# Hybrid decoder step on one core: expert stage fed by quarter rows, transposed on VectorE, multiplied contraction-outer

## What is computed

```python
# per token: one group of 4, then the best 2 of its 8 experts -> 2 x 1088 = 2176 rows to compute
def block(args):
    tok, e = args                      # a block of slots that share one expert
    xb = h[tok]                        # gather rows of 1024 floats
    return (jax.nn.silu(xb @ w1[e]) * (xb @ w3[e])) @ w2[e]    # 1024 -> 512 -> 1024
out = lax.map(block, (slot_tok.reshape(nb, MOE_BLOCK), block_exp))
y = zeros.at[slot_tok].add(out.reshape(-1, D_MODEL) * slot_w[:, None])
```

## Time and profile before

| what | us |
|---|---|
| runs shown, median | 1646.29 |
| the profiled execution, first to last instruction | 1641.5 |
| up products of the first block begin | 997.1 |
| last down product ends | 1585 |
| the next stage's first DMA | 1603.4 |

### The profile page before, as it was taken

The page is one execution under the profiler, slowest core; times in us unless marked ns, Lnnn a source line. Parts: engine busy times, 40 slices in busy tenths (PEclk is TensorE's granted clock), DMA queues, the critical chain, the costliest instruction groups (busy, mean ns, idle before and its releaser), DMA issues. The chain is left out here.

```text
span 1641.5 us, 34661 instructions
## 1 busy us (share of the span) xinstructions
PE 1487.8 (91%) x14240; PEld 979.1 (60%) x14240; DVE 538.9 (33%) x1270; ACT 435.9 (27%) x1227; POOL 290.5 (18%) x250
## 2 busy tenths in 40 slices
PE   8999999989998999999999857999999999999950
PEld 4666666657566677777777433566666655555530
DVE  2445544413325544455444360111111111111106
ACT  2211111131123344434443100222222222222224
POOL 0000000002124333343333001111111111111115
PEclk9999999989998999999999977999999999999985
DMA  7332233242316122221221187999999999999975
GB/s 257 87 94 70 67 81 81 55 147 82 108 63 247 33 78 103 88 99 46 78 84 40 64 350 275 350 384 375 380 377 371 384 368 384 385 378 382 381 265 217
DMA packets 120115, 334.71 MB, mean 204 GB/s; under 512 B 42808, under 2 KB 72424, under 8 KB 92648
## 3 DMA queue, kind: packets, MB, share of 16 engines
q1 hardware_dynamic: 111160, 306.88, 50.4%
q0 software_dynamic: 7728, 22.29, 5.8%
q10 hardware_dynamic: 1152, 4.52, 0.7%
HBM read 290.37 MB, written 48.14 MB: 206 GB/s over the span
## 5 line engine op out<-in xcount | busy, mean ns | idle before, releaser
L2191 PE MATMUL bank<-sb_arena 128*32 128x256 f32 x6336 | 357.3, 386 | 12.9 <-DMA sb_arena<-w 11.8
L398 PE MATMUL bank<-sb_arena 128*128 128x368 f32 x1056 | 330.6, 476 | 6.7 <-DMA sb_arena<-xT 6.7
L2191 PEld LDWEIGHTS bank<-sb_arena 128*32 128x32 f32 x6336 | 205.1, 112 | 153.9 <-DMA sb_arena<-w 13.8
L398 PEld LDWEIGHTS bank<-sb_arena 128*128 128x128 f32 x1056 | 201.7, 191 | 133.5 <-DMA sb_arena<-w_conv 6.7
L2214 PE MATMUL bank<-sb_arena 128*32 128x256 f32 x3168 | 177.1, 379 | 2.0 <-DMA sb_arena<-w 1.0
L2214 PEld LDWEIGHTS bank<-sb_arena 128*32 128x32 f32 x3168 | 102.7, 110 | 70.7 <-issue 2.5
L985 PE MATMUL bank<-sb_arena 128*128 128x512 f32 (+1 forms) x288 | 131.2, 595 | 6.3 <-DVE sb_rlog L1596 5.0
L2157 POOL DMA_INDIRECT d_acc<-sb_arena,sb_oidx x32 | 46.2, 1444 | 472.1 <-ACT sb_arena L2280 472.1
L2330 DVE SCALAR_TENSOR_TENSOR sb_arena<-sb_arena,bank 128x128 f32<-128x128 f32 x99 | 28.6, 288 | 297.3 <-ACT sb_arena L2266 297.3
L2266 ACT ACTIVATE sb_arena<-bank 128x128 f32<-128x128 f32 x99 | 27.5, 278 | 353.6 <-PE bank L2191 353.6
L782 PE MATMUL bank<-sb_arena 128*128 128x384 f32 (+1 forms) x288 | 96.5, 488 | 7.7 <-PEq L151 7.7
(11 more groups left out here) (346 smaller groups left out, 1750.0 us busy)
## 6 DMA issues: line engine op xcount, KB each, us to landing
sb_arena<-w SPq DMA_DIRECT2D x204, 1024.0 KB, 30.5
sb_arena<-w_conv SPq DMA_DIRECT2D x28, 512.0 KB, 4.7
sb_arena<-d_conv SPq DMA_DIRECT2D x7, 1792.0 KB, 7.3
d_conv<-sb_arena SPq DMA_DIRECT2D x22, 512.0 KB, 3.3
sb_arena<-d_gam SPq DMA_DIRECT2D x8, 768.0 KB, 4.1
d_x<-sb_arena SPq DMA_DIRECT2D x9, 512.0 KB, 2.6
sb_arena<-xT ACTq DMA_DIRECT2D x8, 552.0 KB, 9.6
sb_arena<-w_out SPq DMA_DIRECT2D x8, 512.0 KB, 7.0
```

The costliest lines, as they stand in the source:

```text
L398: last = e.matmul(bank[3 * r + s][:, 0:TN], wring[n % NV][:, k, :], xT[:, k, TN * s:TN * s + TN], start=(k == 0), stop=(k == KT - 1))
L2191: mm = e.matmul(bank[r][j * CG:(j + 1) * CG, 0:2 * P], xgT[:, k, g * CG:(g + 1) * CG], w13[s][quarter_of(j, r)][:, k, :], start=(k == 0), ...
```

## The change

**Rows.** A row of `d_x1` or `d_acc` is handled as four pieces of 1 KB. Partition 32*j + i of group r holds quarter j of slot 32*r + i. `xg` and `eo` become 128 partitions x 3 groups x 256. Each gather is three indirect DMAs of 128 pieces, each scatter is three as well, each of them waiting for its own third (`e_eo0` to `e_eo2`). The index table `slot` is spread over 128 partitions in the routing stage: 12 small products and four VectorE operations take the place of seven VectorE operations, and the value is 4 * row + quarter.

**Transposes.** VectorE transposes blocks of 32 x 32 from SBUF to SBUF: `x_flip` (128 x 768) and `h_flip` (128 x 384). TensorE's 11 transposes and ScalarE's three copies of each block go. The weights are laid out in DRAM to match the order of contraction that this gives.

**Products.** `up` runs over four pieces of w13, each of which is now a quarter of the contraction, and all three groups of rows are summed in three PSUM banks side by side; `e_up` counts quarters. `down` does the same with two halves of w2. Numbers and shapes of products are the same (96 and 48, 128 x 32 by 256). `tanh` and `gate` become one instruction each for all three groups, after the whole up product; the gate weight is applied at eviction. TensorE's step is `up(b)`, `down(b-1)`. VectorE's step is `x_flip(b+1)`, `take(b+2)`, `gate(b)`, `mark(b-1)`, `h_flip(b)`.

```diff
-                for ex in range(NSET, E):
-                    for q in (0, 1, 3, 2):
-                        e.wait_ge(S["e_up"], 3 * (ex - NSET) + min(q, 2) + 1)
+                for ex in range(NSET, E):
+                    for q in range(4):
+                        e.wait_ge(S["e_up"], 4 * (ex - NSET) + q + 1)
                         load13(q, ex % NSET, a["w13"][ex, q])
...
                 def gather(index):
                     e.wait_ge(S["e_go"], 1)
                     e.wait_ge(S["e_idx"], index)
-                    e.indirect_dma_start(xg[0:BLK], None, a["d_x1"], bass.IndirectOffsetOnAxis(ap=idx[:, 0:1], axis=0),
-                                         bounds_check=TO - 1, oob_is_err=False).then_inc(S["e_x"], 16)
+                    for r in range(NR):
+                        e.indirect_dma_start(xg[:, r, :], None, rows_in, bass.IndirectOffsetOnAxis(ap=idx[:, r:r + 1], axis=0),
+                                             bounds_check=4 * TO - 1, oob_is_err=False).then_inc(S["e_x"], 16)
...
+                def scatter(n):
+                    for r in range(NR):
+                        e.wait_ge(S["e_go"], 1)
+                        e.wait_ge(S[f"e_eo{r}"], n)
+                        e.indirect_dma_start(rows_out, bass.IndirectOffsetOnAxis(ap=oidx[:, r:r + 1], axis=0), eo[:, r, :], None, compute_op=ALU.add).then_inc(S["e_st"], 16)
...
+                def up(n, s, load, first=False):
+                    e.wait_ge(S["e_xT"], n + 1)
                     if not first:
+                        e.wait_ge(S["e_hm"], n)
+                    for q in range(4):
+                        e.wait_ge(W["w13" + "abcd"[q] + str(s)], 16 * load)
+                        for k in range(2):
+                            for r in range(NR):
+                                for j in range(4):
+                                    mm = e.matmul(bank[UPB + r][j * CG:(j + 1) * CG, 0:2 * P], xgT[:, 2 * q + k, r * CG:(r + 1) * CG], w13[s][q][:, k, j, :],
+                                                  start=(q == 0 and k == 0), stop=(q == 3 and k == 1))
                         mm.then_inc(S["e_up"], 1)
...
+                def x_flip(n, first=False):
+                    e.wait_ge(S["e_x"], 48 * n + 48)
+                    if not first:
+                        e.wait_ge(S["e_up"], 4 * n)
+                    e.transpose(xgT.rearrange("p k (r b) -> p k r b", b=CG), xg.rearrange("p r (k b) -> p k r b", b=CG)).then_inc(S["e_xT"], 1)
...
+                def h_flip(n, first=False):
+                    e.wait_ge(S["e_hm"], n + 1)
+                    if not first:
+                        e.wait_ge(S["e_out"], 2 * n)
+                    e.transpose(hT.rearrange("p r c -> p (r c)"), hm.rearrange("p r c -> p (r c)")).then_inc(S["e_hT"], 1)
...
                 with e.Fori(1, last + 1) as b:
+                    x_flip(e.snap(b + 1))
                     take(e.snap(b + 2))
                     gate(b)
                     mark(e.snap(b - 1))
+                    h_flip(b)
```

More of the change, by code:

```diff
@@ L1890, in program @@
         A = Arena()
-        w13 = [[A(P, KT, 2 * P) for _ in range(4)] for _ in range(NSET)]
-        w2 = [[A(P, DE // P, 512) for _ in range(2)] for _ in range(NSET)]
+        w13 = [[A(P, 2, 4, 2 * P) for _ in range(4)] for _ in range(NSET)]
+        w2 = [[A(P, 2, D) for _ in range(2)] for _ in range(NSET)]
         ohp = A(P, 2 * NTT, BLK)
@@ L1956, in _ @@
                     last = e.matmul(bank[2][0:BLK, 0:3 * NBMAX], ohp[:, m, :], ohb[:, m, :, :].rearrange("p a b -> p (a b)"), start=(m == 0), stop=(m == 2 * NTT - 1))
+                last.then_inc(S["r_pe"], 1)
+                e.wait_ge(S["r_sub"], 6)
+                for r in range(NR):
+                    for j in range(P // CG):
+                        last = e.matmul(bank[3][j * CG:(j + 1) * CG, r * 2 * NBMAX:(r + 1) * 2 * NBMAX], ident[0:BLK, r * CG:(r + 1) * CG],
+                                        listed[0:BLK].rearrange("p a n -> p (a n)"), start=True, stop=True)
                 last.then_inc(S["r_pe"], 1)
@@ L2174, in _ @@
                 last = last_block(e)
-                def x_transpose(n, first=False):
-                    e.wait_ge(S["e_x"], 16 * n + 16)
+                def up(n, s, load, first=False):
+                    e.wait_ge(S["e_xT"], n + 1)
                     if not first:
-                        e.wait_ge(S["e_xT"], n)
-                    for k in range(KT):
-                        mm = e.transpose(bank[3 + k // 4][:, (k % 4) * BLK:(k % 4 + 1) * BLK], xg[0:BLK, k * P:(k + 1) * P], ident[0:BLK, 0:BLK])
-                    mm.then_inc(S["e_xT_ps"], 1)
@@ new lines, in down @@
+                        e.wait_ge(S[f"e_eo{r}"], n + 3)
+                    for h in range(2):
+                        e.wait_ge(W["w2" + "ab"[h] + str(s)], 16 * load)
+                        for k in range(2):
+                            c = 2 * h + k
+                            for r in range(NR):
+                                for j in range(4):
+                                    mm = e.matmul(bank[OUT + r][j * CG:(j + 1) * CG, 0:256], hT[:, r, c * CG:(c + 1) * CG], w2[s][h][:, k, j * 256:(j + 1) * 256],
+                                                  start=(c == 0), stop=(c == 3))
@@ L2233, in _ @@
                 with e.Fori(E, last + 1) as b:
-                    before = e.snap(b - 1)
-                    h_transpose(before)
-                    x_transpose(e.snap(b + 1))
                     up(b, UP_SET, b)
-                    down(before, DOWN_SET, b)
-                h_transpose(last)
+                    down(e.snap(b - 1), DOWN_SET, b)
                 down(last, UP_SET, E // NSET + 1)
@@ L2251, in _, with tanh @@
                 last = last_block(e)
-                def x_copy(n, first=False):
-                    e.wait_ge(S["e_xT_ps"], n + 1)
+                def tanh(n, first=False):
+                    e.wait_ge(S["e_up"], 4 * n + 4)
                     if not first:
-                        e.wait_ge(S["e_up"], 3 * n)
-                    for s in range(2):
-                        copy = e.activation(xgT[:, 4 * s:4 * s + 4, :].rearrange("p k n -> p (k n)"), bank[3 + s][:, 0:4 * BLK], ACT.Copy)
-                    copy.then_inc(S["e_xT"], 1)
@@ L2309, in _ @@
+                copy.then_inc(S["e_eo2"], 1)
             @block.vector
@@ L2341, in _ @@
                 e.memset(eo, 0.0).then_inc(S["e_go"], 1)
+                x_flip(0, first=True)
                 take(1)
+                x_flip(1)
+                take(2)
                 gate(0, first=True)
-                take(2)
+                h_flip(0, first=True)
                 with e.Fori(1, last + 1) as b:
+                    x_flip(e.snap(b + 1))
                     take(e.snap(b + 2))
```

215 lines of the change are left out of this document (80 added, 135 removed).

## The result

The changed kernel takes 1626.07 us (median of four runs, 1622.40 to 1628.14), the kernel before 1645.78 beside it. The ratio is 0.9886, 95% interval 0.9867 to 0.9906. The profiled executions differ by 1641.5 - 1623.7 = 17.8 us. The forecast was 1637: the direction was right, the gain is twice as large as forecast.

A forecast was written before the change was run, and what follows sets the result against it. The DMA engines were taken as the bound, at 18.3 us a block. Pieces -3, start -3 and end -3 made -9 us on 1641.5, so 1632.5; with 4.8 us from profiled span to median, 1637, range 1615 to 1690.

The forecast's parts named there:

- Part 1: TensorE's transposes and ScalarE's copies go, 1.14 us a block; counted as nothing because the DMA engines hide them.
- Part 2: Gather and scatter in 1 KB pieces: DMA work and imbalance net -0.1 us a block, -3 us over 31 blocks.
- disturbance: Weight rows beside the 96-partition gather take 0.358 us each, against 0.315 alone; expected gone with a 128-partition gather.
- imbalance: Empty slots on the last partitions load some DMA engines more: 0.3 us a block, 0.2 taken as gone.
- small pieces: 1 KB pieces on the DMA engines: gather 0.8 us a block against 0.75, scatter 2.4 against 1.96, queue changes 0.2.
- Part 3: GpSimd issues six DMAs a block instead of two, 7.3 to 9.7 us, hidden under 18.3 us.
- Rival 2: The gather's round trip becomes the bound, deciding once issue and landing take over 17 us; slower, 1668 us, chance 0.10.
- Part 4: VectorE's block transposes take 0.8 and 0.45 us, at most twice that; VectorE and ScalarE work stays hidden.
- Part 5: Stage start: the second up product no longer waits for the third block's gather; -4 us, with longer routing -3.
- Part 6: Stage end: less product remains after the last w13 piece, against a longer scatter issue; -3 us, bounds +4 and -6.
- Rival 1: Each small scatter piece costs a toll, deciding from 0.12 us; up to +5 us a block, likelier 1668 us, chance 0.30.
- Rival 3: Imbalance and disturbance both vanish and small pieces are free: -0.6 us a block, 1621 us with start and end, chance 0.15.

The follow-up runs named there:

- light products: Half of the contraction left out of both products, all DMAs whole: 1612.67 us on the changed kernel, 1635.63 us on the kernel before.
- light weight loads: Each weight DMA of the stage moves only 1 KB of every 8 KB row: 1574.59 us on the changed kernel, 1618.72 us on the kernel before.
- tiny: The changed kernel with each of its three gathers replaced by a plain DMA of 16 bytes a partition: 1611.44 us beside 1643.24.
- late gather: The changed kernel with `take(b + 2)` put behind `h_flip(b)`: 1702.01 us beside 1646.21.

## Why the prediction was partly right

**The bound.** "The DMA engines run flat out throughout": right for both kernels by the share. The 18.3 us a block are the mean of twelve late blocks, the last two of which (16.8 and 17.2 us) were hardly held up; with light products it is 18.5. What failed for the changed kernel is that this bound stays. Late blocks were to come 18.2 us apart with TensorE waiting for weights in almost every one. TensorE never waits for them, and the blocks come 16.88 us apart. The 18.2 us appear only with light products. The rule that every microsecond of DMA work counts 31 times comes out near: 17.9 - 18.34 = -0.45 us x 31 = -14 by the rates, and 17.2 were measured. In part that is luck, since TensorE's own rate sets the pace of the changed kernel.

**Part 1, transposes at nothing.** Right for the kernel before (5 us), wrong for what follows from it. "A block of 15.7 us" would have been 15.54, but with stops it is 16.9. The part had no price for the case that the DMA bound falls away; there it is 28 us.

**Part 2, the step that failed.** It put the DMA work of a block at 0.1 us less than before; the runs show 0.3 less (18.2 against 18.5 with light products) to 0.45 less (389 against 379 GB/s). The packet times were right: the added piece is 0.102 us (forecast 0.10; from 1291 to 1299 us, beside a scatter, 0.33 MB take 26.0% of 16 x 8 us), the weights' rows 85.5% x 16 x 194 us / 8269 = 0.321 or 15.4 us a block (forecast 15.3, with 0.005 us for a change of queue that no row or run shows), the rows' queue 3.2 (forecast 3.2 and 0.1 of semaphore writes). Their sum of 18.6 us was forecast and came, and it was still no block time. It goes with a share of 1.045 where it had been 1.02, and it is a mean over the engines. In the terms of the sum: the disturbance was booked at 0.7 us a block (15.8 less 15.1) and is 0.8 to 1.0 by the rates; the imbalance at 0.2, and the spread slots give 0.29; the small pieces at 0.05 + 0.44 + 0.2 = 0.69, and the measured difference leaves 0.5 (401 against 389 GB/s) to 1.0 (1.0 + 0.3 - 0.3), so about what was booked. The forecast's sum also held 0.1 us of semaphore writes that its parts before (0.75 + 1.96) did not, hence -0.1 and not -0.2. Net it was 0.2 to 0.35 us a block too small, times 31 some 6 to 11 of the 14 us that the middle missed. The rest is not resolved by term. The prediction held the 128-partition gather for a side effect of the small pieces; alone it is worth 15 us, and the small pieces cost.

**Part 3, GpSimd hidden.** Its six issues take 8 us a block (70.52 of 150 us, 8.9 blocks), within the forecast of 7.3 to 9.7. It was hidden as an engine, but its scatters stand in the rows' round trip of 16.8 us. Rival 2 named such a round trip for the gather and put its threshold over 17; it missed the longer one over scatter, `mark` and copy. It came within 0.1 us of deciding.

**Part 4.** The flips take 0.98 and 0.58 us (forecast 0.8 and 0.45, at most twice that), hidden.

**Part 5, the start.** The reason was right: the second product no longer waits for the third block's gather. It comes at 1011.08, not 1019, after a wait of 2.69 us for `gate`, and the share up to 1048 us is 0.96, not 0.79. 9.6 us instead of 3. The longer routing did not show: the first product comes at 996.14, against 997.11.

**Part 6, the end, has the wrong sign.** The forecast counted the last weight piece; but TensorE did not wait for weights, so nothing of that was gained. Two things came instead. TensorE ends 4.8 us later after the last `up` than before: both products stretch with the stops, the last `down` waits 2.55 us for the copy, which waits for the scatter before, and it takes 7.07 us instead of 5.39. Behind that wait the granted clock is 0.65 from 1556 to 1560 us, a mixture of its two levels (1.2 and 2.4 GHz), where it had been 1.00. Then the last copy begins 8.5 us after TensorE's end, where it had been 4.6: it waits 7.57 us for three scatter DMAs that land 12 us after the last issue, where it had waited 4.20. The three issues of the last scatter, 3.7 us longer than one, cost nothing: from the first of them to the next stage it is 12.5 us in both kernels.

**The rivals.** Rival 1, a toll on each small piece, fell with the 0.102 us of an added piece (it decided from 0.12); its price by its own terms, 0.17 x 24 + 1.8, is 5.9 us and not 5. Rival 2 was a limit that did not decide, as told under part 3. Three DMAs instead of one did cost time in the chains: the three issues take 1.04 us (gather) and 1.57 us (scatter) each, in a row, and the last copy's wait for the landing grew by 3.4 us. The Trainium skill puts a fixed cost of some 2 us on each DMA ("DMA: Bandwidth & Descriptors", Anatomy of one DMA). No run here measures that cost by itself. Rival 3, with disturbance and imbalance gone, gave 1621; with the forecast's 1637 about as far above, the measured 1626 lies between them, nearer to the rival.

## What to carry to other kernels

In this kernel an indirect gather on 96 partitions beside full-width loads took 5% of the DMA rate (401 to 379 GB/s), and empty slots that always lie on the same partitions took 0.29 us of 18.3 a block. Both losses go with an index beyond the bound and another deal of the slots, without touching the layout. Sum DMA work for the slowest engine, not for the mean, and read a loss off the rate in GB/s rather than off packet times. When a bound is lowered, price every hidden part again without its cover: here the transposes cost 28 us, and the scatter's round trip (16.8 us) was within 0.1 us of TensorE's 16.9.

## What the runs showed of the hardware

- The gather's 1 KB pieces are recorded as packets of 4 KB. The queues of the changed kernel from 1300 to 1303 us, a gather beside the weights, first the counts by size:

```profile
DMA packets 239, 1.28 MB, mean 426 GB/s; under 512 B 51, under 2 KB 51, under 8 KB 115
...
q1 hardware_dynamic: 140, 1.02, 80.7%
q0 software_dynamic: 99, 0.26, 21.9%
```

No packet lies between 512 B and 2 KB, 64 between 2 and 8 KB; they carry the 0.26 MB in at most 0.164 us each (21.9% of 16 x 3 us / 64). The forecast's 264 pieces at 0.047 us came to nearly the same time by luck. Which four pieces share a packet the trace does not show; by the code, neighbouring partitions take the same quarter of different rows. In the scatter the pieces stay apart (0.33 MB in 326 packets from 1291 to 1299 us).
- TensorE's stops: two to three of 0.4 to 0.6 us, a few instructions behind the end of `down`. With eleven transposes in between they stand at the end of `down` and in the transposes, not in `up`. They are gone with light weight loads, with a tiny or a late gather and, in most blocks, with empty pieces left out, and a fourth gather DMA adds a fourth. Loads of instructions do not pair with them: the queues of kind "instruction" moved 3 packets from 1340 to 1534 us, against 34 stops. What stops TensorE is open.
